# Attention of a hybrid encoder layer: value products in two column groups, probabilities summed by GpSimd and VectorE, and a narrower product for the rotary key

## What is computed

```python
q = (_rms_norm(cq, q_norm_g) @ w_uq)      # 8 heads x (64 + 32)
q_nope, q_rope = q[..., :64], _apply_rope(q[..., 64:], cos, sin)
kv = (_rms_norm(ckv, kv_norm_g) @ w_ukv)  # 8 heads x (64 + 64): k_nope, v
k_rope = _apply_rope(k_rope, cos, sin)    # one rotary key of 32, shared by the heads
s = q_nope . k_nope + q_rope . k_rope     # per head, 1024 x 1024
p = softmax(s * 96 ** -0.5)
o = p @ v                                  # 64 wide per head
```

## Time and profile before

| | |
|---|---|
| median of 3 runs | 1607.21 us (1605.63 to 1608.45) |
| the profiled execution's own time | 1606.11 us |
| its span | 1604.3 us |
| mean granted TensorE clock | 0.98 |
| busy: PE, PEld, DVE, ACT, POOL | 1519.6, 1023.6, 1047.6, 715.8, 364.7 us |

### The profile page before, as it was taken

The page is one execution under the profiler, slowest core; times in us unless marked ns, Lnnn a source line. Parts: engine busy times, 40 slices in busy tenths (PEclk is TensorE's granted clock), DMA queues, the critical chain, the costliest instruction groups (busy, mean ns, idle before and its releaser), DMA issues.

```text
span 1604.3 us, 15464 instructions
## 1 busy us (share of the span) xinstructions
PE 1519.6 (95%) x5730; PEld 1023.6 (64%) x5730; DVE 1047.6 (65%) x1028; ACT 715.8 (45%) x696; POOL 364.7 (23%) x195
## 2 busy tenths in 40 slices
PE   6999999999999999999999990799999999999997
PEld 3444587844344445555558870688888888888774
DVE  4533235433733564777756558599998998999886
ACT  3311000035412114344442432477777777777773
POOL 0031000000011003144545324022332222332204
PEclk9999999999999999999999995899999999999999
DMA  9311130207000000000022329699999999999995
GB/s 314 127 53 53 38 120 1 56 7 140 26 0 1 0 0 27 1 13 14 27 105 81 109 87 379 232 361 378 378 378 372 374 378 378 378 378 376 369 381 203
DMA packets 152885, 284.41 MB, mean 177 GB/s; under 512 B 25300, under 2 KB 35874, under 8 KB 152835
## 3 DMA queue, kind: packets, MB, share of 16 engines
q1 hardware_dynamic: 147219, 263.28, 46.2%
q0 software_dynamic: 4464, 16.25, 3.8%
q10 hardware_dynamic: 1152, 4.19, 0.6%
HBM read 259.07 MB, written 24.64 MB: 177 GB/s over the span
## 4 chain that ended last, share of the span: by engine, by line
PE 85%; DVE 5%; DMA 4%; ACT 3%; issue 2%; POOL 0%; SPq 0%; POOLq 0%; DVEq 0%; ACTq 0%
PE psum L1138 15%; PE psum L1551 9%; PE psum L1553 9%; PE psum L1552 9%; PE psum L1415 6%; PE psum L1351 4%; PE psum L1206 3%; PE psum L1119 3%; DMA arena<-in_exp_w_down 3%; PE psum L1321 2%; PE psum L1084 2%; PE psum L1462 2%; PE psum L1222 2%; PE psum L1221 2%; PE psum L1464 2%
## 5 line engine op out<-in xcount | busy, mean ns | idle before, releaser
L2032 DVE TENSOR_TENSOR split_at<-arena,split_at 128x2048 fp32r<-128x2048 f32 x188 | 427.9, 2290 | 60.1 <-ACT split_at L1000 58.7
L1000 ACT ACTIVATE split_at<-arena 128x2048 fp32r<-128x2048 f32 x192 | 367.6, 1915 | 67.5 <-PE psum L1553 53.2
L1551 PE MATMUL psum<-split_at,split_at 128*128 128x512 f32 x768 | 305.9, 398 | 1.4 <-DVE split_at L2038 1.4
L1553 PE MATMUL psum<-split_at,split_at 128*128 128x512 f32 x768 | 300.2, 391 | 0.0
L1552 PE MATMUL psum<-split_at,split_at 128*128 128x512 f32 x768 | 299.5, 390 | 0.0
L1138 PE MATMUL psum<-arena 128*128 128x512 f32 (+1 forms) x544 | 238.6, 594 | 0.0
L1138 PEld LDWEIGHTS psum<-arena 128*128 128x128 f32 (+1 forms) x544 | 99.5, 185 | 132.9 <-issue 132.8
L1553 PEld LDWEIGHTS psum<-split_at,split_at 128*128 128x128 f32 x768 | 144.5, 188 | 31.2
L1551 PEld LDWEIGHTS psum<-split_at,split_at 128*128 128x128 f32 x768 | 144.7, 188 | 29.7 <-DVE split_at L2038 1.8
L1552 PEld LDWEIGHTS psum<-split_at,split_at 128*128 128x128 f32 x768 | 144.9, 189 | 28.3
L1415 PE MATMUL psum<-arena 128*128 128x512 f32 x256 | 120.8, 594 | 3.7 <-ACT arena L893 2.8
(11 more groups left out here) (300 smaller groups left out, 2142.1 us busy)
## 6 DMA issues: line engine op xcount, KB each, us to landing
arena<-in_exp_w_gate SPq DMA_DIRECT2D x64, 1024.0 KB, 14.3
arena<-in_exp_w_up SPq DMA_DIRECT2D x64, 1024.0 KB, 14.2
arena<-in_exp_w_down SPq DMA_DIRECT2D x64, 1024.0 KB, 14.2
arena<-in_w_in SPq DMA_DIRECT2D x9, 1024.0 KB, 8.4
arena<-in_x SPq DMA_DIRECT2D x8, 512.0 KB, 6.6
xhat_scratch<-arena SPq DMA_DIRECT2D x8, 512.0 KB, 9.6
arena<-in_w_out SPq DMA_DIRECT2D x8, 512.0 KB, 3.6
arena<-xhat_scratch SPq DMA_DIRECT2D x8, 512.0 KB, 4.9
```

Of the source, the lines that this page charges most:

```text
L1000: a(flat(wsplit[c % WS][0]), wraw[:, c], ACT.Copy).then_inc(s_whi, 1)
L1551: mm(bank(out_bank), src[0][:, k, :], whi[:, k % 4, :], start=(k == 0), stop=False)
L1553: ins = mm(bank(out_bank), src[1][:, k, :], whi[:, k % 4, :], start=False, stop=(k == KT - 1))
L2032: tt(flat(lo), wraw[:, c], flat(hi), ALU.subtract).then_inc(s_wlo, 1)
```

## The change

It has three parts.

1. The value product takes 64 columns (`v_at` itself, without ones), and the two halves of the queries go to partitions 0 to 63 and 64 to 127 of one bank. Two key blocks are scored one after the other, and then two value products are issued one after the other. There are four probability buffers.
2. The sums come from additions: POOL adds the probabilities of blocks 0 to 3 of a head (three additions, L882's outputs), DVE those of blocks 4 to 7, and PE multiplies both by 64 columns of ones (`sum_probs`) into bank 7. DVE takes the reciprocals straight from that bank, in two pieces of 128 x 256 (`sums_inverse`), and scales 64 x 512 at a time. The copy of v is gone. The loads of two gains and of the stored input move to later places.
3. The rotary key's projection alternates between two column groups of 32 (even slices to partitions 64 to 95, odd ones to 96 to 127) in one piece (`project_key`). A small matrix product sums the two and another turns them (`key_partners`).

```diff
-        rot = mem(784, 128)
+        rot_in = mem(784, P + 2 * DR)
+        rot, key_sum, key_turn = rot_in[:, 0:P], rot_in[:, P:P + DR], rot_in[:, P + DR:]
-        v1 = mem(43984, 2, KT, 2 * DV)
-        p_at = mem(46032, 2, T)
-        o_raw = mem(30672, 2, T)
-        o_inv = mem(52176, 2, 256, p1=DV)
+        p_at = mem(43984, 4, T)
+        p_first, p_last = mem(27600, T), mem(29648, T)
+        o_raw, o_inv = mem(30672, 2, HALF), mem(52176, 2, HALF)
...
-        MAX_FIRST = {2: 0, 3: 2, 4: 4, 5: 6}
-        MAX_SECOND = {2: 1, 3: 3, 4: 5, 5: 7}
-        ROWS_AT = 6
+        ROUGH_AT = {(0, 0): (0,), (0, 1): (1,), (0, 2): (2,), (1, 0): (3,), (1, 1): (4,), (1, 2): (5,), (2, 0): (6,), (2, 1): (7,)}
+        ROUGH_AT_0 = {(0, 2): (0,), (1, 0): (1,), (1, 1): (2,), (1, 2): (3, 4), (2, 0): (5,), (2, 1): (6,), (2, 2): (7,)}
...
-            sp.wait_ge(s_vs, NH)
-            for dst, src in ((gin, A["ln_in_g"]), (bin_, A["ln_in_b"]), (gmix, A["ln_mix_g"][0]), (bmix, A["ln_mix_b"][0])):
+            sp.wait_ge(s_exp, TT * (NH - 1))
+            for dst, src in ((gin, A["ln_in_g"]), (bin_, A["ln_in_b"])):
                 sp.dma_start(dst, src.partition_broadcast(P)).then_inc(s_gb, 16)
-            for i in range(2):
-                sp.dma_start(xres[:, i, :], xh_tok[:, i, :]).then_inc(s_xh[i], 16)
-            sp.wait_ge(s_ov, N_PAIR)
+            sp.dma_start(xres[:, 0, :], xh_tok[:, 0, :]).then_inc(s_xh[0], 16)
+            sp.wait_ge(s_gb, 32)
+            sp.wait_ge(s_sum, 2 * NH)
+            sp.dma_start(xres[:, 1, :], xh_tok[:, 1, :]).then_inc(s_xh[1], 16)
+            for dst, src in ((gmix, A["ln_mix_g"][0]), (bmix, A["ln_mix_b"][0])):
+                sp.dma_start(dst, src.partition_broadcast(P)).then_inc(s_gb, 16)
+            sp.wait_ge(s_ov, N_OUT + 4)
...
+            def add_probs(h, i):
+                pool.wait_ge(s_exp, TT * h + i + 2)
+                if i == 0 and h:
+                    pool.wait_ge(s_sum, 2 * h - 1)
+                if i:
+                    pool.wait_ge(s_pa, 3 * h + i)
+                first = p_at[:, 0, :] if i == 0 else p_first
+                pool.tensor_tensor(p_first, first, p_at[:, i + 1, :], ALU.add).then_inc(s_pa, 1)
             for h in range(NH):
-                if h + 1 < NH:
+                if h and h + 1 < NH:
                     head_low(h + 1, 0)
                     head_low(h + 1, 1)
-                if h >= 1 and h + 1 < NH:
-                    v_copy(h + 1)
+                for i in range(3):
+                    add_probs(h, i)
+                if h == 0:
+                    head_low(1, 0)
+                    head_low(1, 1)
...
             def probs(n):
+                h, kb = divmod(n, TT)
                 act.wait_ge(s_qk, n + 1)
-                if n >= 2:
-                    act.wait_ge(s_pv, n - 1)
-                a(p_at[:, n % 2, :], bank(2 * (n % 2), 2), ACT.Exp).then_inc(s_exp, 1)
+                if n >= 4:
+                    act.wait_ge(s_pv, n - 3)
+                    if kb >= 4:
+                        act.wait_ge(s_pa, 3 * h + max(kb - 4, 1))
+                    else:
+                        act.wait_ge(s_da, 3 * h - 3 + max(kb, 1))
+                a(p_at[:, n % 4, :], bank(2 * (n % 2), 2), ACT.Exp).then_inc(s_exp, 1)
...
-                if n + 1 < N_UNIT:
-                    probs(n + 1)
+                probs(n)
...
+            def project_key():
...
+                for j in range(2):
+                    for k in range(KT):
+                        p0 = DV + DR * (k % 2)
+                        ins = mm(bank(proj_bank(I_KR) + j, 1, p0, p0 + DR), win_w[c][:, k, 0:DR], xT[:, k, HALF * j:HALF * j + HALF],
+                                 start=(k < 2), stop=(k >= KT - 2))
+            def key_partners():
...
+                for b, mat in ((0, key_turn), (2, key_sum)):
+                    for j in range(2):
+                        ins = mm(bank(b + j, 1, DV, DQ), mat[DV:P, :], kr[DV:P, HALF * j:HALF * j + HALF], start=True, stop=True)
...
-            project(I_KR, 0, 4)
+            project_key()
             gates(2, 0)
             sum_squares(0)
-            project(I_KR, 4, 5)
-            project(I_KR, 5, 7)
+            project(I_CQ, 0, 3)
             gates(2, 1)
-            project(I_KR, 7, 8)
-            project(I_CQ, 0, 2)
...
-            for j in range(2):
-                ins = mm(bank(j), rot, kr[:, HALF * j:HALF * j + HALF], start=True, stop=True)
-            ins.then_inc(s_krm, 1)
-            project(I_CQ, 2, 6)
+            project(I_CQ, 3, 5)
+            key_partners()
+            project(I_CQ, 5, 6)
+            project(I_CQ, 6, 8)
             pe.wait_ge(s_kro, 1)
             gates(3, 0)
-            project(I_CQ, 6, 8)
-            project(I_CQ + 1, 0, 1)
+            project(I_CQ + 1, 0, 3)
...
-                    ins = mm(bank(6 + j), v1[:, h % 2, kb, :], p_at[:, n % 2, HALF * j:HALF * j + HALF], start=(kb == 0), stop=(kb == TT - 1))
+                    ins = mm(bank(6, 1, DV * j, DV * j + DV), v_at[:, kb, DV * h:DV * h + DV], p_at[:, n % 4, HALF * j:HALF * j + HALF],
+                             start=(kb == 0), stop=(kb == TT - 1))
+            def sum_probs(h, part):
+                if part == 0:
+                    pe.wait_ge(s_pa, 3 * h + 3)
+                    if h:
+                        pe.wait_ge(s_oi, 2 * h)
+                else:
+                    pe.wait_ge(s_da, 3 * h + 3)
+                for j in range(2):
+                    ins = mm(bank(7, 1, DV * j, DV * j + DV), ones[:, 0:DV], (p_first, p_last)[part][:, HALF * j:HALF * j + HALF],
+                             start=(part == 0), stop=(part == 1))
+                ins.then_inc(s_sum, 1)
...
+            scores(1)
+            for h in range(NH):
+                more = h + 1 < NH
+                for m in range(4):
+                    n = TT * h + 2 * m
+                    slots = (ROUGH_AT if h else ROUGH_AT_0) if more else {}
+                    if m < 3:
+                        for i in range(2):
+                            scores(n + 2 + i)
+                            for qt in slots.get((m, i), ()):
+                                rough_next(h + 1, qt)
+                        if m == 0 and h:
+                            sum_probs(h - 1, 1)
+                    elif more:
+                        max_turn(h + 1)
+                    pv(n)
+                    pv(n + 1)
+                    for qt in slots.get((m, 2), ()):
+                        rough_next(h + 1, qt)
+                sum_probs(h, 0)
+                if more:
+                    scores(TT * h + TT)
+                    scores(TT * h + TT + 1)
+            sum_probs(NH - 1, 1)
...
+            for h in range(NH):
+                slots = (ROUGH_AT if h else ROUGH_AT_0) if h + 1 < NH else {}
+                if h == 0:
                     rotary_low(1)
+                for m in range(3):
+                    for i in range(3):
+                        for qt in slots.get((m, i), ()):
+                            row_max(h + 1, qt, 4)
+                        if h and (m, i) == (0, 1):
+                            sums_inverse(h - 1, 0)
+                        if h and (m, i) == (1, 1):
+                            sums_inverse(h - 1, 1)
+                add_probs(h, 0)
+                if h + 1 < NH:
+                    max_rows(h + 1)
+                add_probs(h, 1)
+                add_probs(h, 2)
+                if h:
+                    for j in range(2):
+                        o_scale(h - 1, j, 0, HALF)
+            sums_inverse(NH - 1, 0)
+            o_scale(NH - 1, 0, 0, 256)
+            sums_inverse(NH - 1, 1)
+            for j, c in ((0, 1), (1, 0), (1, 1)):
+                o_scale(NH - 1, j, 256 * c, 256 * c + 256)
```

More of the change, by code:

```diff
@@ L48, in shape_constants @@
     rot = np.eye(P)[partner]
+    both = np.tile(np.concatenate([np.eye(DR), rot[0:DR, 0:DR]], axis=1), (P // DR, 1))
     order = np.concatenate([np.arange(0, T, 2), np.arange(1, T, 2)])
@@ L272, in encoder @@
         s_mxa, s_mxau = sem("mix_psum_first"), sem("mix_read_first")
-        s_wo, s_woh, s_wol = [sem(f"w_out_ld{i}") for i in range(2)], sem("w_out_high"), sem("w_out_split")
+        s_wo, s_woh, s_wol = s_x[2:4], sem("w_out_high"), sem("w_out_split")
         s_gb = sem("gains_ld")
         s_rw, s_gff = s_rope, s_mw
-        s_xh = [sem(f"xhat_ld{i}") for i in range(2)]
+        s_xh = s_x[0:2]
         s_res, s_mix, s_mixu, s_x1 = sem("residual"), sem("mix_psum"), sem("mix_read"), sem("x1_done")
@@ L471, in _ @@
             sp.wait_ge(s_z, 8)
-            for dst, name in ((rot, "c_rot"), (cos_t, "c_cos"), (sin_t, "c_sin")):
+            for dst, name in ((rot_in, "c_rot"), (cos_t, "c_cos"), (sin_t, "c_sin")):
                 sp.dma_start(dst, A[name]).then_inc(s_rope, 16)
@@ L834, in _ @@
             act.wait_ge(s_pj, I_KR + 1)
-            act.wait_ge(s_zero, 2)
-            a(kr[DV:DQ, :], bank(proj_bank(I_KR), 2, DV, DQ), ACT.Copy).then_inc(s_pja, 1)
```

(47 more changed lines are left out.)

82 lines of the change are left out of this document (34 added, 48 removed).

## The result

The changed kernel takes 1615.82 us (median of 5 runs, 1614.47 to 1616.77) where the kernel before takes 1607.21: the ratio is 1.0054, 95% interval 1.0039 to 1.0069. It is slower by 8.6 us, and my forecast was 1584, 23 us faster. Its profiled execution has a span of 1614.9 us, against 1604.3.

The account below looks back on a forecast made before the run. PE (TensorE) was taken to bound the kernel, busy 95% of the span. Gains of 18.6 (attention), 1.0 (its end) and 5.0 (rotary key), less 2 allowed, made 22.6 us off 1606.1: 1583.5, given as 1584 against the median; range 1570 to 1606.

Parts of the forecast that it names:

- n/2 + 1 steps: Value products: n narrow passes in a phase take n/2 + 1 steps of 0.43 us; 191 steps, 82.0 us, before 109.9.
- edges of 0.31: Attention on PE: each pair of changes between narrow and full matmuls costs 0.31 us; 31 phases, 9.6 us.
- rival (d): Value products and key: all passes run side by side, 31 + 1 steps less, 13.7 us, total 1570; chance 0.03.
- (a): Column groups on PE: no overlap, passes run one after another, 61.8 us more, total 1646; chance 0.12.
- (b): Column groups on PE: weight loads held at 144 crossings, 0.15 us each, 21.6 us, total 1605; chance 0.13.
- my 7.61: Rotary key's projection: 17 steps and one phase, 7.30 + 0.31 us, against 13.74 plus 0.93 of edges before.
- my 5.0: Rotary key: net gain of 5.0 us, projection and partner product together, with nothing late behind it.
- 2 us in all: DVE in attention: allowance for products of two SBUF operands held beside POOL operations, most heads escaping.
- Rival (c): DVE and POOL hold one another: late row of maxima delays next head's first maximum, 2 us x 6, 1596; chance 0.09.
- PE's 1.0 us for POOL's last split: End of attention: PE's wait for w_out's last split goes, POOL's queue ending at 21.7 us, before PE's 22.9.
- 218.4 + 2: Attention after the change: 218.4 us against 237.0 before, plus 2 us allowed for DVE held by POOL.
- forecast 9.5: PE's waits in attention: 5.3 us in head 0 and 0.7 a head elsewhere, together 9.5, before 9.8.

Follow-up runs that it names:

- e7: Kernel of e1, but both query halves of the value product go to the same 64 columns (timing only): 1629.32 us, ratio 1.0139.
- e4: Kernel before the change with the narrow rotary key alone: 1602.53 us, ratio 0.9976.
- e5: Changed kernel with one more wait: POOL's first addition of a head waits for DVE's scaling products of the head before: 1579.88 us, ratio 0.9827.
- e1: Changed kernel with a head's two scaling products earlier in DVE's queue, after the row maxima of slots (1,2) and (2,0): 1582.88 us, ratio 0.9854.
- e3: Changed kernel with 18 useless matmuls ahead of the second rough product in heads 1 to 6, where PE waits: 1604.55 us, ratio 0.9989.
- e6: Kernel of e1, with the last head's three POOL additions moved to DVE and the last two w_out splits asked for earlier: 1587.58 us, ratio 0.9876.
- e8: Kernel of e5, with w_out block 6's split moved ahead of POOL's additions of head 7 and block 7's earlier: 1583.19 us, ratio 0.9852.

## Why the prediction was wrong

*The value products: cheaper than forecast.* I took n/2 + 1 steps for n passes. Eight passes start at 745.23 and the next rough product at 747.09 in the changed kernel: 1.86 us, with the way out of the narrow form in it, where five steps alone are 2.15. So n passes take n/2 steps: 160 x 0.43 = 68.8 and not 82.0. The edges of 0.31 hold. This is the overlap of rival (d), to which I gave 0.03. Rivals (a) and (b) are out; e7 shows how much hangs on it: without the overlap the kernel takes 1629.

*The rotary key: right but for one wait.* 32 passes took 6.99 us of my 7.61, and its partner product 3.54 of 3.74 (417.21 to 420.75 in the changed kernel). I wrote that DVE's rotation comes later and nothing waits; PE waits 1.36 for DVE (the new row at L1138 in e4). Attention starts 4.8 us earlier in the changed kernel (599.16 against 603.95) and the time gains 3.8 in e4, for my 5.0.

*The other engines: here it failed.* The step that failed is "POOL's split of head h+2 starts at about 23.0, 0.3 us after the addition, so most heads escape; I allow 2 us in all". I followed DVE's queue only to the row of maxima. That one is indeed in time (720.69). Behind it stand two additions and two scaling products, and behind these the next head's first maximum, for which PE has no buffer to go on. By rows taken without POOL they are 2 x 1.23 + 2 x 0.7 = 3.9 us, and end at about 725.8, before the rough product at 727.18. Beside POOL's two splits and its three additions they take 11.0, and the maximum is 5 us late. In place of my 2 us in all, PE's waits there are 24.6 us and come with 14.6 us of slower clock; against e5 the difference is 35.0. The trace of before had a sign of it: the 28 scaling products in its attention (L1909) take 888 ns on average, not the 0.42 of one alone, 13 us in all, and no PE wait for DVE stands in attention. DVE was held before the change too, and nothing that PE needed in time was queued behind. Rival (c) had the right pair of engines, and it even named the next head's first maximum. But it let that come only from a late row of maxima, which the changed kernel does not show, at 2 us a head instead of about 7 in each of heads 2 to 6, with a chance of 0.09; the runs show e1's and e5's 33 to 36 us.

The Trainium skill ("Trainium Architecture — The Big Picture", What this means for kernel authors) calls the port pair that the two engines share "an exclusive lock (not a bandwidth split)". The traces agree in their sizes: a product of 0.7 us takes 2.8 beside a chain of additions of 2.66, not 1.4. They do not agree for POOL's operation on a single tensor (L600, see the last section).

*What I had no term for: the clock.* All rows of before in attention were at 1.00, and I priced idle time as idle time only. At each of the five waits of 4.8 to 5.1 us a stretch of some 6.8 us at 1.2 GHz follows or begins just before the wait ends. That is 14.6 us of the 35, by e5 against the change, and 15.9 by e3. In e3 the narrow products and the late maximum are as in the change, and only the idle time is filled: so the clock follows the idle time.

*The end of attention.* I wrote that PE's 1.0 us for POOL's last split goes. It became 1.9. PE arrives 1.2 us earlier in the head than I reckoned (21.7 instead of 22.9, by the passes), and POOL's splits take 11.9 instead of 10.4: two of their four operations last longer beside DVE's (3.81 and 2.78 us for 2.85 and 2.39). Behind the wait 3.4 us are at 1.2 GHz, some 1.7 us more.

*The sum.* By the profiled spans the error is 33.2 us (1614.9 for a forecast of 1581.7). The forecast for attention was 218.4 + 2. With e5's order it is 212.65: 13.2 less for the passes, and 7.4 more in waits and short gaps (115.5 + 78.4 + 1.8 leaves 17.0, forecast 9.5), of which the view of the waits names 5.5, 1.3 and 1.3. With the order of the change it is 35.0 more, and the change is a loss. So 27.3 us of the error lie in attention (247.7 for 220.4), and the hand-over between DVE and POOL at the change of heads is more than all of it. Another 5.8 lie behind attention, where 763.3 us became 768.1 and I had taken 1.0 off: the wait for POOL is 1.9 of them and the clock behind it some 1.7. The other 2.2 I cannot place; e5 has 768.5 there too, so they are no part of the hand-over.

What stays open: how much of those 7.4 us belongs to the one bank pair of the rough products (a rough product follows the last by 2.04 us where matmuls between them fill 1.87), and whether an order exists in which the last head has neither the wait for POOL nor one for DVE; e6 and e8 missed it.

## What to carry to other kernels

When work moves to a second elementwise engine, write out both queues around every instruction with two SBUF inputs and look at what is queued behind it, not only at the instruction that has a deadline: here a short DVE product took as long as the POOL addition or split beside it lasted, and a chain of POOL additions held one product after another. Start the chain behind the short products (one wait here gave 36 us), or put these where POOL is idle. And price an idle stretch of a busy TensorE at more than its length, if the trace shows the clock fall after it: here 20.4 us of idle time cost 14.6 more.

## What was not expected of the hardware

- Two float32 matmuls (two passes each) in two column groups of 64 overlap wholly: eight passes in 1.86 us with the edge, where eight passes in one group took 3.57 in e7 (717.07 to 720.64). The same for groups of 32 (32 passes in 6.99).
- DVE's row maximum, which reads PSUM, stayed at 1217 ns on average in 56 instances, beside the same POOL work that held the SBUF products.
- A wait of 1.9 us of PE at the start of the mixer is followed by matmuls at 1.2 GHz (0.63 us a record). Neither wait of 1.3 in head 0 is: the clock is 1.00 behind both.
- Not every POOL operation held DVE. The ones that did (splits, additions, residuals) are TENSOR_TENSOR. Beside POOL's TENSOR_SCALAR on 128x1024 (L600, 836.70 to 839.55 in the changed kernel) a DVE addition at 837.75 took 1.23 us, as alone, and beside the next one (842.01 to 845.82) a scaling product at 845.1 took 0.7, though an addition at 843.2 took 1.95.
